# Weight tiles loaded in one 1 MB transfer each, with shorter waits at six places of the order

## What is computed

```python
# first block: differential attention, then sliding-window attention with sinks
q, k, v, gate = jnp.split(h @ w_in, 4, axis=-1)          # a_w_in  [2048, 8192]
x + (rms_norm(attention) * silu(gate)) @ w_out           # a_w_out [2048, 2048]
k_sh, v_sh = jnp.split(rms_norm(x) @ w_kv, 2, axis=-1)   # w_kv    [2048, 512]
q, gate = jnp.split(rms_norm(x, norm_g) @ w_in, 2)       # b_w_in  [2048, 4096]
x + (o * jax.nn.silu(gate)) @ w_out                      # b_w_out [2048, 2048]
# second block: stick-breaking, forgetting and RWKV-7 branches, then an MLP
proj = u @ w_in                                          # [2048, 12580]
m = g_a * (y_a @ w_branch_a) + g_b * (y_b @ w_branch_b) + g_c * (y_c @ w_branch_c)
x = x + _rms_norm(m @ w_out, norm_mix_post)
hdn = jnp.square(jax.nn.relu(_rms_norm(x) @ w_mlp_up))   # [2048, 8192]
x = x + _rms_norm(hdn @ w_mlp_down, norm_mlp_post)       # [8192, 2048]
```

## Time and profile before

| | |
|---|---|
| median of 3 runs | 2513.26 us |
| lowest and highest | 2512.82 and 2513.78 us |
| the profiled execution's own time | 2514.11 us |
| span of its trace | 2512.3 us |
| granted TensorE clock | 0.999 of full speed |
| PE busy | 99% of the span |
| weight load of PE (PEld) busy | 90% |
| POOL, ACT and DVE busy | 75%, 50% and 40% |
| DMA queue q1, share of 16 engines | 55.5% |
| weights loaded | 782 DMAs of 512 KB, 3.6 us each to landing (median) |

### The profile page before, as it was taken

How to read it: one execution, slowest core, us unless ns; L and a number is a source line. 1 busy time by engine, 2 the same in 40 slices (tenths; PEclk the granted TensorE clock), 3 DMA queues, 4 the chain that set the end, 5 groups by cost and what they waited for, 6 DMA issues and landing times.

```text
span 2512.3 us, 48968 instructions
## 1 busy us (share of the span) xinstructions
PE 2492.0 (99%) x19776; PEld 2271.0 (90%) x19776; DVE 1010.9 (40%) x1648; ACT 1257.7 (50%) x1608; POOL 1882.2 (75%) x781
## 2 busy tenths in 40 slices
PE   9999999999999999999999999999999999999998
PEld 9999999999888899899999999998888888888886
DVE  6455454326665441226454454342651220220322
ACT  5554454566776655454435353446553443443543
POOL 4777777777666887676666675888798888888886
PEclk9999999999999999999999999999999999999999
DMA  6455555555554666455455454566566666666665
GB/s 239 142 160 151 152 159 155 156 168 152 152 150 139 189 186 206 143 171 155 141 152 150 144 152 136 168 194 210 158 191 182 181 200 195 184 194 190 184 190 163
DMA packets 119371, 426.20 MB, mean 170 GB/s; under 512 B 12816, under 2 KB 17040, under 8 KB 118928
## 3 DMA queue, kind: packets, MB, share of 16 engines
q1 hardware_dynamic: 114336, 416.58, 55.5%
q10 hardware_dynamic: 4848, 6.82, 0.8%
HBM read 419.15 MB, written 4.19 MB: 169 GB/s over the span
## 4 chain that ended last, share of the span: by engine, by line
PE 52%; POOL 25%; issue 21%; DVE 1%; ACT 1%; POOLq 0%; DVEq 0%
POOL wl L3284 25%; PE ps L244 10%; PE ps L252 5%; PE ps L227 5%; PE ps L225 5%; PE ps L234 5%; PE ps L283 5%; PE ps L293 5%; PE ps L285 5%; PE ps L382 2%; PE ps L378 2%; PE ps L377 2%; PE ps L391 1%; PE ps L1000 1%; PE ps L396 0%
## 5 line engine op out<-in xcount | busy, mean ns | idle before, releaser
L3284 POOL TENSOR_TENSOR wl<-raw,wh 128x1024 fp32r<-128x1024 f32 x775 | 1877.2, 2445 | 615.3 <-ACT wh L206 612.8
L206 ACT ACTIVATE wh<-raw 128x2048 fp32r<-128x2048 f32 x390 | 745.9, 1913 | 628.9 <-DMA raw<-weights 216.1
L244 PE MATMUL ps<-hp,wh 128*128 128x512 f32 x1520 | 373.6, 396 | 2.0 <-ACT wh L206 2.0
L244 PEld LDWEIGHTS ps<-hp,wh 128*128 128x128 f32 x1520 | 279.0, 188 | 65.1 <-issue 5.8
L225 PE MATMUL ps<-hp,wh 128*128 128x272 f32 (+2 forms) x1152 | 287.8, 287 | 0.0
L227 PE MATMUL ps<-hp,wh 128*128 128x272 f32 (+2 forms) x1152 | 286.7, 286 | 0.0
L391 PE MATMUL ps<-hp,wh 128*128 128x256 f32 x1792 | 233.8, 285 | 1.8 <-DVE og L2098 1.8
L391 PEld LDWEIGHTS ps<-hp,wh 128*128 128x128 f32 x1792 | 218.2, 189 | 9.3 <-issue 4.7
L227 PEld LDWEIGHTS ps<-hp,wh 128*128 128x128 f32 (+1 forms) x1152 | 216.6, 188 | 0.1
L225 PEld LDWEIGHTS ps<-hp,wh 128*128 128x128 f32 (+1 forms) x1152 | 215.9, 187 | 0.2
L252 PEld LDWEIGHTS ps<-hp,wl 128*128 128x128 f32 x1520 | 191.9, 188 | 9.5 <-POOL wl L3284 1.2
(11 more groups left out here) (515 smaller groups left out, 3777.2 us busy)
## 6 DMA issues: line engine op xcount, KB each, us to landing
raw<-weights SPq DMA_DIRECT2D x782, 512.0 KB, 3.6
xT<-tokens SPq DMA_DIRECT2D x4, 544.0 KB, 6.6
spill<-xT ACTq DMA_DIRECT2D x1, 2048.0 KB, 13.2
xT<-spill ACTq DMA_DIRECT2D x1, 2048.0 KB, 9.9
C<-consts SPq DMA_DIRECT2D x1, 2032.0 KB, 14.8
arena<-lora ACTq DMA_DIRECT2D x4, 384.0 KB, 3.3
arena<-rows ACTq DMA_DIRECT2D x1, 1024.0 KB, 6.3
out<-arena SPq DMA_DIRECT2D x2, 512.0 KB, 2.6
```

Source lines behind the costliest of these rows:

```text
L206: nc.scalar.activation(wh[:, m % 2, :, :].rearrange("p a b -> p (a b)"), raw[:, 2 * (m % 2):2 * (m % 2) + 2, :, :].rearrange("p a b c -> p ...
L244: return nc.tensor.matmul(both, wh[:, slot, kt, :], pair[:, :, kt, 0:SEQ], start=(kt == 0), stop=(kt == KT - 1))
L3284: nc.gpsimd.tensor_tensor(wl[:, s // 2, h, :], raw[:, s, :, :], wh[:, s // 2, h, :].bitcast(F32), ALU.subtract)\
```

## The change

Eight edits. The first is to the loads, the others to the order.

- SP loads a tile in one DMA of 1 MB, issued when both halves of its buffer have been read, where it issued two of 512 KB, each when its own half had been read. The counts that `round_weights` and the third mlp tile wait for follow.
- `wide_tile` does 13 `high` products ahead of the first eight `wl` products, and the 14th and 15th behind these eight.
- `opening_two` cuts its second tile at `kt` 10.
- In the b stretch DVE's remainder of a quarter of `og` comes one step earlier.
- In the last round, the fill parts 86 and 87 come ahead of the matmul of the variance.
- The `land` steps 5, 7 and 8 come earlier in DVE's order.
- The last piece of `PIECES` is cut in two, and a wait that it had is gone.
- In the hidden tiles of the mlp, ACT rounds the next tile behind its first copy, ahead of the wait for DVE's sum.

```diff
-            act.wait_ge(raw_in[m % 2], 32 * (m // 2 + 1) + 16 * per * i)
+            act.wait_ge(raw_in[m % 2], 16 * (m // 2 + 2) + 8 * per * i)
...
-            for kt in range(KT - 1):
+            for kt in range(KT - 3):
                 high(kt)
             for kt in range(KT):
+                if kt == 8:
+                    high(KT - 3)
+                    high(KT - 2)
                 if kt % 8 == 0:
                     pe.wait_ge(lo_done, 2 * q + kt // 8 + 1)
...
-            for kts in (range(12), range(12, KT)):
+            for early, late in ((True, False), (False, True)):
                 for t, acc in enumerate(accs):
+                    cut = (12, 10)[t]
+                    kts = range(cut) if early else range(cut, KT)
...
-                if s in (6, 10, 14):
+                if s in (5, 9, 13):
                     split_bo.quarter_dve(dve, s // 4 - 1)
...
                     low_rank(i + 1)
+                else:
+                    fill(pe, i, range(86, 88))
                 pe.wait_ge(A.sem, A.at("sqy", i))
                 mm(ps[:, 4, :], c("hones"), tmp["t1"].rearrange("p a b -> p (a b)"))\
                     .then_inc(T.sem, T.step("var"))
-                fill(pe, i, range(86, 88))
                 if i < ROUNDS - 1:
+                    fill(pe, i, range(86, 88))
...
+                land(dve, i, 5)
                 dve.wait_ge(T.sem, T.at("bon", i))
...
-                land(dve, i, 5)
...
+                    if step in (1, 2):
+                        land(dve, i, 6 + step)
...
-                    if step != 1:
-                        land(dve, i, {0: 7, 2: 8, 3: 9, 4: 10}[step])
+                    if step >= 3:
+                        land(dve, i, 6 + step)
...
-                  (range(10, 12), 3), (range(12, 16), 4))
+                  (range(10, 12), 3), (range(12, 14), 4), (range(14, 16), 5))
...
-                if k == LAST:
-                    dve.wait_ge(V.sem, V.at("l3"))
...
                         nc.scalar.activation(fu["r"][:, t % 4, :], ps[:, t % 4, SEQ:2 * SEQ], ACT.Copy).then_inc(SHC, 1)
+                    if i or t >= 2:
+                        round_weights(act, "mlp", t + 2, i, 32)
+                    if i or t >= 3:
                         act.wait_ge(SJ, halves_joined(i, t))
...
-                    if i or t >= 2:
-                        round_weights(act, "mlp", t + 2, i, 32)
...
-                sp.dma_start(raw[:, slot, :, :].rearrange("p a b -> p (a b)").unsqueeze(1),
-                             w[:, bass.ds(n, 1), :]).then_inc(raw_in[slot // 2], 16)
+                sp.dma_start(raw[:, 2 * slot:2 * slot + 2, :, :].rearrange("p s a b -> p s (a b)"),
+                             w[:, bass.ds(n, 2), :]).then_inc(raw_in[slot], 16)
             with sp.Fori(1, N_TILES // 2) as i:
-                for s in range(4):
-
-                    sp.wait_ge(lo_done, 4 * i + s - 3)
-                    load(4 * i + s, s)
+                for slot in range(2):
+
+                    sp.wait_ge(lo_done, 4 * i + 2 * slot - 2)
+                    load(4 * i + 2 * slot, slot)
```

More of the change, by code:

```diff
@@ L331, in opening_two @@
                                                stop=(kt == 15))
-                    if kts[-1] == KT - 1:
+                    if late:
                         ins.then_inc(tile_done, 1)
@@ L2846, in mix_act @@
                     m, half = FIRST["mlp"] + 2, k - 1
-                    act.wait_ge(raw_in[m % 2], 32 * (m // 2 + 1))
+                    act.wait_ge(raw_in[m % 2], 16 * (m // 2 + 2))
                     act.wait_ge(tile_done, done("bc", 7))
@@ L3204, in load @@
             def load(n, slot):
-                sp.dma_start(raw[:, slot, :, :].rearrange("p a b -> p (a b)").unsqueeze(1),
-                             w[:, bass.ds(n, 1), :]).then_inc(raw_in[slot // 2], 16)
+                sp.dma_start(raw[:, 2 * slot:2 * slot + 2, :, :].rearrange("p s a b -> p s (a b)"),
+                             w[:, bass.ds(n, 2), :]).then_inc(raw_in[slot], 16)
             with sp.Fori(1, N_TILES // 2) as i:
-                for s in range(4):
-                    sp.wait_ge(lo_done, 4 * i + s - 3)
-                    load(4 * i + s, s)
-            for s in range(2 * (N_TILES % 2)):
-                sp.wait_ge(lo_done, 4 * (N_TILES // 2) + s - 3)
-                load(4 * (N_TILES // 2) + s, s)
+                for slot in range(2):
+                    sp.wait_ge(lo_done, 4 * i + 2 * slot - 2)
+                    load(4 * i + 2 * slot, slot)
+            if N_TILES % 2:
+                sp.wait_ge(lo_done, 4 * (N_TILES // 2) - 2)
+                load(4 * (N_TILES // 2), 0)
             for b, pieces in enumerate((2, 4)):
```

## The result

The changed kernel takes 2590.32 us (median of 6 runs, 2584.51 to 2593.04), against 2513.21 before (6 runs, 2512.71 to 2513.78). The ratio is 1.0301, with a 95% interval of 1.0291 to 1.0311: 77 us slower. The forecast was 41 us slower, 2554, with a range of 2522 to 2596. The direction and the mechanism held. The size was underestimated by nearly half, and what came out is close to rival (c), though not for the reason that (c) gave.

What follows compares the result with a forecast made beforehand. PE, busy 99%, bounds the kernel, with the weight buffers' chain 0.7 us behind in two tiles. Loads lose 46 us, the order gains 5: 41 more than the profiled 2514.1, median 2554, range 2522 to 2596.

Steps and rivals of the forecast that it cites:

- rival (c): Transfer at the run's mean rate, 1.75 us: chain 12.25, total 2592; upper end of the 2531 to 2592 given 0.72.
- The rule to batch to 1 MiB: Loads: DMAs of at least 1 MiB for 75% of peak rate; speaks for the edit, but nobody pays the fixed part.
- the table: Loads: the skill page's listing of 6.15 us for a 1 MB DMA, which would give some 2680 us.
- the fit: Loads: 2.0 us plus bytes at 436 GB/s; second 512 KB costs 1.2 us, loss 41 in place of 46.
- The order's gain in the rounds: Rounds: 1.0 us gained at the last round's variance, up to 1.8 from the earlier `land` steps.
- The rest, stretch by stretch: Loads' loss by stretch at 5.88 us a tile, less reserves, plus late landings: 46 us in all.
- The mlp, 50.8 in place of 34.7: Mlp, 124 tiles: 34.7 us from pitch 5.88 against 5.60, less 3.5 and 1.5, gives 29.7; late landings add 5.0.
- Late landings: Mlp: each landing beyond the median now delays the chain; estimated 0.04 us a tile, 5.0 us.
- The reserve: POOL's lead over PE, spent once a stretch: 1.5 us off mlp, 0.5 mix_out, 1.5 gates and bc, 2.5 zz, 1.0 b_out.
- The order: Edits to the engines' order remove waits of PE in last round, `land`, mlp and elsewhere: 5 us gained, between 1 and 7.
- The lower bound of 1.0 for the second 512 KB: Loads: landing medians at 384 and 512 KB, being rounded, allow as little as 1.0 us, against the 1.26 taken.
- the signs: Profile after: landings 4.6 to 5.0 us, ACT released by transfers, POOL 74% busy, PE waiting 0.2 to 0.4 us each mlp tile.

Runs made afterwards that it cites:

- The experiment with one operand: Kernel with the 1 MB transfer alone, DVE's two-operand subtraction in the mlp's hidden tiles replaced by a one-operand multiplication by a constant: 2590.47 us, ratio 1.0307.

## Why the prediction was right in kind and short in size

**Right.** PE sets the end before the change, and the buffers' chain stands 0.7 us behind it in two tiles; the 1 MB transfer costs 1.26 us more (3.71 to 4.97 us from POOL's end in the mlp, with the kernel that has this edit alone); two token tiles then take 11.76 us, ACT is released by the transfer, POOL is busy 73% (74 forecast), and the first 500 us are unchanged. The rule to batch to 1 MiB, which the forecast weighed (the Trainium skill, page "DMA: Bandwidth & Descriptors", section "Bandwidth"), does hold for the efficiency of the queue (its share falls from 55.5% to 46.8%), and the trace agrees with the forecast that nobody was paying for that. The rule, the table and the fit that the forecast took from this page stand there for DMAs issued from GpSimd, and these loads are issued by SP; the forecast didn't say so. The order's gain in the rounds (2.8 forecast) came out at 3.5.

**Short, by 38 us of the loads' 84.** The step that fell short is "The rest, stretch by stretch": the pitch of the token tiles was right, but single tiles were lost that no term stood for, and some terms were put too low.

1. *The mlp, 50.8 in place of 34.7.* The hidden tiles' chain was put at POOL's 4.77, read while DVE's product slipped in behind a tile's second subtraction. Once the chain bounds, the phases shift, it slips in between the two, and from ACT's start to POOL's end it is 6.94 us in place of 6.75: two tiles in 11.9. The experiment with one operand gives 4 us of this back. The last token pass lost 11.2 us where 4.5 were forecast: DVE's work on the output stands beside POOL's there, and single subtractions take 3.4 us in place of 2.4.
2. *Late landings, put at 0.04 us a tile and only in the mlp.* In the kernel with the 1 MB transfer alone 31 transfers land later than 5.1 us. The 12 of the mlp that are over 5.0 are 11.7 us over 4.8 together, twice the 5.0 of the forecast, and those in zz (up to 8.7) and mix_out (up to 8.0) are paid there as well. Those two stretches were 13 us over the forecast. But zz's 10.1 us stand in two tiles: 4.5 at the late landing, and 5.7 at the opening, where no transfer was late. The 2.5 that I had put down there for the pitch were not lost.
3. *The reserve.* I took 1.5, 0.5, 1.5, 2.5 and 1.0 us off for the distance between POOL's end and PE's need. In the mlp every second tile is at PE's minimum (5.60) and the next takes the whole rest of the two (6.1 to 6.6, and over 7 where a landing was late). So a disturbance that before fell into the reserve is now on the path. This is argued; no run measures what the reserve gave back.
4. *The openings and the clock, put at zero.* kv, where I had put nothing, lost 2.1, all in its first tile, where DVE's remainders stood behind POOL and PE waited for them; its other three tiles (6.97, 6.00 and 6.00 us) are what they were. zz's first tile lost 5.7 in the same way, 3.4 of them, as an estimate, by half clock. I had priced the chain of the weights alone, and not what a POOL that works later does to the DVE steps that PE waits for at the start of a stretch. No experiment takes this out by itself.

Rival (c) gave 2592 for a transfer at the run's mean rate (1.75 us). The time is right and the reason isn't: the transfer went at the full queue's rate. So the rival's number is met by luck, and a time that fits doesn't confirm the rival that names it. The range held for the same reason: it was drawn for another price of the transfer, and what filled it was something else.

**The order.** 5 us forecast, 1.8 measured with the loads of before: 1.9 gained at mlp tile 5 (1.3 forecast), 3.5 in the rounds (2.8 forecast) and 0.6 at the end of b; against them 2.5 lost at mlp tiles 10 to 14, which wasn't foreseen, and 0.02 us in each hidden tile, over 1 us in the mlp, where `wide_tile` was put at 0. With the square moved 4.8 come out.

**Smaller slips in the working.** PE's longest single wait before is 1.4 us, at the very start of the run, and not 1.3. At bc's pitch of 5.70 a tile loses 0.18 us and not 0.23. The lower bound of 1.0 for the second 512 KB allows less than the rounding of its rows does (3.35 to 3.55 us would give 0.8). And PE does not wait 0.2 to 0.4 us at each mlp tile, as the signs had it: its waits for ACT's L206 and POOL's L3292 that are shown above come 54 times in the whole run.

## What to carry to other kernels

Before a change to the loads, add up the loop that one buffer runs through (transfer, every reader, next issue) and compare it with the consumer's time for as many tiles as there are buffers; a transfer's efficiency counts only where the queue is full. Where that loop comes within a few per cent of the consumer's time, price each disturbance in full and not only the mean, and read the loop's parts again as they will stand to each other after the shift. Ask also what else the later engine will stand in the way of, above all where PE waits for a short step at the start of a stretch. And of an instruction that is moved forward ask what stands ahead of it in its new place: one wait for a slow sum undid the gain of the early rounding.

## What the runs showed of the hardware

- *Late landings go with packets of other queues.* With the 1 MB transfer alone, of 389 weight transfers 171 had packets of another queue between their issue and their landing, and all 31 that landed later than 5.1 us are among these; of the 218 with none, not one. In the changed kernel it is 33 of 35. The two longest (8.7 and 8.0 us) ran beside some 1800 and 1900 packets of queue q10. Mostly it is a single 16 KB packet of the instruction queue. For a transfer that landed in 6.03 us in the changed kernel (2091.3 to 2097.4 us):

```profile
q1 hardware_dynamic: 144, 1.05, 51.4%
q8 instruction: 1, 0.02, 1.0%
```

One such packet goes with 1.2 us here; but with the 1 MB transfer alone 140 others with a packet beside them weren't late, so it isn't enough by itself. What else it takes is open.
- *Without slack the runs of a kernel spread.* The kernel before agrees within 1.1 us in the six runs beside the changed one (within 3.0 to 5.2 in 13 to 21 runs beside the experiments). The changed one spreads over 10.6 us in ten (2584.14 to 2594.78), and the one that POOL's shorter work sets free over 0.6 in ten. It isn't a sure sign: the two kernels with the order's edits and the square in its old place, which PE bounds, spread over 5.6 us in ten runs and 6.4 in eleven. A part of the spread goes with the clock: the four runs of the 1 MB transfer alone took 2593.51, 2596.18, 2597.97 and 2601.59 us at a mean granted clock of 0.998, 0.997, 0.996 and 0.994.
- *A wait of PE can cost twice.* Behind PE's waits of 2.1 us at 911.6 and 3.0 at 979.0, and of 1.8 and 0.95 at 1813.8 and 1815.8, the granted clock was 0.50 for 6.8, 3.4 and 3.4 us (1 MB transfer alone). Behind the 1.8 us at kv and the 1.3 us of the kernel before it stayed at full speed.
- *A DVE instruction that waits for POOL is shown as a long one.* Its 128 x 256 subtraction has 0.81 to 1.99 us in these rows, where one ahead of zz that nothing stands beside takes 0.42; the 128 x 1024 sum has 1.21 us free and 3.42 behind a POOL pair that ends 2.3 us after its start (1830.14 + 4.95 against 1832.75). POOL pays less: 0.20 us in its pair for the subtraction, in the rows shown.
